# A hybrid decoder step on one core: one half of an SSM table moved to an earlier group, and the C and state rows loaded in an earlier block

## The chip, the cores and the metric

One NeuronCore of a Trainium2 chip runs the whole program, in float32. The metric is device time in microseconds of one execution; lower is better. Before the change it was 1676.16 us, the median of three runs (1675.69 to 1676.87).

## The reference, cut to what matters

The program is one step of a decoder layer for 1024 prompt tokens and 32 sample tokens (8 sequences of 4). A combined projection feeds two token mixers, their outputs are gated and projected, and a mixture of experts follows.

```
proj = h @ w_in                                   # u (512) | q, k, v (3 groups x 4 heads x 64)
# SSM branch: x_t = Abar x_(t-1) + Bbar u_t, y = Re(C x) + D u
dt = exp(log_step); mag = exp(lr*dt); ab = mag*cos(li*dt) + i*mag*sin(li*dt)
bb = (ab - 1) / (lr + i*li) * b                   # complex, 32 groups x 64 states x 16 channels
# sample tokens start from state_ssm_re/_im (8, 32, 64); prompt tokens from zero
# attention: three groups, window 128/512/2048 and dilation 1/4/16, prompt and sample
w = softmax over the three groups of their log-sum-exp
attn = sum_g w_g * o_g
gates = sigmoid(h @ w_mgate + b_mgate)
merged = g_ssm * (ssm @ w_br_ssm) + g_attn * (attn @ w_br_attn)
x = x + gt1 * (merged @ w_out); x = x + gt2 * moe(norm(x)); y = rmsnorm(x)
```

The kernel handles the scan in chunks of L = 8 tokens. For it, it needs powers of Abar (0 to 8), a table "ba" of Abar^(7-j) Bbar (the input table: what each of the 8 tokens of a chunk injects into the state; real part `ba_re`, imaginary part `ba_im`, 128 x 2048 each), and a table "ca" of C Abar^j.

## The kernel before, in words

The kernel is written engine by engine in blocks. All engines meet at the end of a block, so nothing of the next block starts before the slowest engine has finished this one. Within a block each engine works through its own list in the order written; semaphores join the lists. Four blocks matter here.

- **Projection block** (before 431 us): normalisation and the combined projection.
- **Prompt attention block** (lines 623 to 783). 24 units (3 groups x 8 tiles of 128 queries) go through PE (scores, transposed probabilities, values), DVE (mask, row maximum, half of the copies) and ACT (exponentials, other copies). SP loads two slabs of gate weights and then, for each unit, waits for the unit's output rows and stores them (L781). The rows sit in a ring of OB = 4 buffers `o_sb`; from unit 4 on, DVE's row maximum (L732, it writes into `o_sb`) waits until the store of four units before has landed. POOL writes zeros into the expert buffer (L634) and stores values (L650, L653).
- **Sample attention block** (lines 884 to 1299), the one that the change is about. Its parts:
  - SP starts it with the loads of the SSM parameters (L898 to L900, L903), then 32 loads of rows of C (L907), 2 loads of state rows (L910), and the caches of K and V of sample group 0 (L891). Later caches wait for the earlier group's use. After group 2 it stores the last sample rows, loads the rows of attention results of all tokens into `merge` (L928, L931).
  - PE has gate units as filler: `fill(step)` (L969) runs `FILL[step]` units of 8 matmuls of 128x352 at fixed points of its list, 30 units in all. Two units come first ("start"), then the transpose of the parameters (L976), one unit ("params"), then the wait for the 32 loads of C and the 2 of the states, their six transposes (L981, L983), three units ("c_h0"), and then for each sample group g: cache transposes (L997), scores (L1012, L1014), transposes (L1020, L1021, L1025, L1026), values (L1034, L1036), the transpose of the rows (L1041), with one unit in between each time. After group 2 nine units follow ("merge" 5, "merged" 4), then PE waits for the merged rows (`s_mrg`) and transposes them (L1052).
  - DVE computes the SSM constants, copies C and states out of PSUM (L1096 to L1099), and in each group does its copies and softmax steps. After the copy of the transposed probabilities (L1187, L1188) it runs one SSM piece: `powers` in group 0, `b_bar` in group 1, `b_table_re` in group 2. The adding of values (L1191) comes after the piece. After group 2: L1193, a memset (L1194), `b_table_im`, the chain table `e` (squarings and complex products, L1200 to L1221), then the merge of the three groups' rows (L1223 to L1245) and the copies of their transposes (L1249). The helper `tt` of L1061 records most of the products, so they all show as L1061.
  - POOL computes the table "ca" (L949 to L954) as soon as powers and C are there. ACT applies the bias to every gate unit and stores it (L1262, L1265), and computes the exponentials and sines between.
- **SSM block** (from L1340): transposes of the inputs, taps, injection with the tables `ba`, scan, output. The branch projections, router and experts follow in further blocks.

`big` is one buffer of 128 x 19584 that the stages share by column ranges. In the prompt attention, columns 0 to 18815 hold q, k and v. In the sample attention the turned caches `kct` use 14816 to 18911, and DVE's scratch for the tables is 10720 to 12767.

Of the kernel before, what the change touches and what calls it, by code (L numbers as in the profile page):

```python
# [38 lines left out]
SP2 = SSM_G // 2  # L39
# [36 lines left out]
def build(nc, I, O, scratch):  # L76
    ctx = ExitStack()
    with ctx:
# [5 lines left out]
        def sem(name):  # L84
            if front_sems is not None:
                s = nc.alloc_semaphore(name)
                front_sems.append(s)
                return s
            return ctx.enter_context(nc.semaphore(name))
# [15 lines left out]
        big = sb("big", [P, 19584])  # L105
# [37 lines left out]
        for blk in order:  # L143
            first_unit[blk] = len(units)
            kind, b = blk
# [452 lines left out]
        def place(rows, g, t):  # L598
# [4 lines left out]
                return rows[512 * (t // 4) + t % 4:512 * (t // 4 + 1):4]  # L603
            return rows[t:SEQ:8]

        OB = 4
        s_sc, s_msk, s_nm, s_p = sem("scores_in_psum"), sem("scores_masked"), sem("row_max_ready"), sem("probs_ready")
        s_gw = [sem(f"gate_weights{i}_loaded") for i in range(2)]
        s_zr, s_zst, s_vst = sem("zero_rows_ready"), sem("zero_rows_stored"), sem("v_stored")
        s_pt, s_pta, s_ptd = sem("probs_t_in_psum"), sem("probs_t_copied_act"), sem("probs_t_copied_dve")  # L610
        s_pv, s_o, s_st = sem("values_in_psum"), sem("values_copied"), [sem(f"att_rows_stored{i}") for i in range(OB)]

# [4 lines left out]
        with ExitStack() as st:  # L617
            s_sb = sb("s_sb", [P, 2, HEADS, 2 * P], stack=st)
            p_sb = sb("p_sb", [P, 2, HEADS, 2 * P], stack=st)
            pt_sb = sb("pt_sb", [P, 2, 2, HEADS, P], stack=st)  # L620
            o_sb = sb("o_sb", [P, OB, HEADS, HD + 2], stack=st)

            with nc.Block() as block:  # L623
# [91 lines left out]
                def _(dve):  # L715
                    V = nc.vector
                    for i in range(NU + 1):
                        if i < NU:
# [10 lines left out]
                            dve.wait_ge(s_msk, i + 1)  # L729
                            if i >= OB:  # L730
                                dve.wait_ge(s_st[i % OB], 16 * (i // OB))
                            V.tensor_reduce(o_sb[:, i % OB, :, HD].rearrange("p (k r) -> p r k", r=2),  # L732
                                            s_sb[:, i % 2, :, 0:w], AX.X, ALU.max, negate=True).then_inc(s_nm, 1)
# [10 lines left out]
                def _(act):  # L744
                    A = nc.scalar
                    for i in range(NU + 2):
                        if i < NU:
# [4 lines left out]
                            for s in range(HEADS):  # L752
                                h = 2 * (s % 2) + s // 2
                                m = A.activation(p_sb[:, i % 2, s, 0:w], s_sb[:, i % 2, s, 0:w], ACT.Exp,  # L754
                                                 bias=o_sb[:, i % OB, h, HD:HD + 1], scale=1.0,
                                                 accum_out=o_sb[:, i % OB, h, HD + 1:HD + 2])
# [15 lines left out]
                @block.sync  # L772
                def _(sp):
                    for b in range(2):
                        sp.dma_start(ring[:, b, :].rearrange("p (k c) -> p k c", k=KT),
                                     I["w_mgate"][0][:, b * WB:(b + 1) * WB].rearrange("(k p) c -> p k c", p=P)).then_inc(s_gw[b], 16)
                    for u, (g, t) in enumerate(att):
                        sp.wait_ge(s_o, u + 1)
                        sp.wait_ge(s_p, u + 1)
                        dst = place(scratch["att_rows"].rearrange("n g h d -> n g (h d)")[:, g, :], g, t)  # L780
                        sp.dma_start(dst, o_sb[:, u % OB, :, :].rearrange("p h d -> p (h d)")).then_inc(s_st[u % OB], 16)  # L781
                    for i in range(OB):
                        sp.wait_ge(s_st[i], 16 * NU // OB)
# [49 lines left out]
                                            sem("max_factors"), sem("merged"))  # L833
        s_atp, s_ate = sem("attn_t_in_psum"), sem("attn_t_copied")
        s_dve3, s_pool3 = sem("dve_chain3"), sem("pool_chain3")
        s_pl, s_bl, s_cl, s_hl = sem("ssm_params_loaded"), sem("ssm_b_loaded"), sem("ssm_c_loaded"), sem("ssm_h0_loaded")
        s_dtr, s_pt4, s_ct4 = sem("step_rows_ready"), sem("params_in_psum"), sem("c_in_psum")
        s_a1, s_a2, s_a3, s_a4 = sem("dt_ready"), sem("exponents_ready"), sem("magnitudes_ready"), sem("angles_ready")
        s_a5 = sem("sines_ready")
# [15 lines left out]
        with ExitStack() as st:  # L855
# [2 lines left out]
            rp = big[:, 1536:1792].rearrange("p (i j n) -> p i j n", i=2, j=L)  # L858
            par_rows = big[0:48, 1792:1920]
            ls = big[0:48, 1920:1922]  # L860
            h_rows4 = big[:, 10432:10688].rearrange("p (a c) -> p a c", a=2)
            c_rows4 = big[:, 18912:19424].rearrange("p (a c) -> p a c", a=4)
            g_sb = sb("gate_units", [P, GB, CW], stack=st)
            vc = sb("vc", [P, 4096], stack=st)
            st_sb = sb("st_sb", [P, 3, P], stack=st)
# [18 lines left out]
            with nc.Block() as block:  # L884
                @block.sync
                def _(sp):
                    def load_cache(src, dst, s, g):
                        rows = src[0].rearrange("n s h d -> n s (h d)")
                        if g < 2:
                            for b in range(KB[g]):  # L890
                                sp.dma_start(dst[:, :, b, :], rows[:, b * P:(b + 1) * P, :].rearrange("n s c -> s n c")).then_inc(s, 16)  # L891
                        else:

                            for a in range(16):
                                sp.dma_start(dst[4 * a:4 * a + 4, :, 0, :],
                                             rows[:, 16 * a:16 * a + 4, :].rearrange("n s c -> s n c")).then_inc(s, 16)

                    sp.dma_start(par_rows[0:16, :], I["ssm_a_re"][0].rearrange("(n r) s -> n (r s)", r=2)).then_inc(s_pl, 16)  # L898
                    sp.dma_start(par_rows[16:32, :], I["ssm_a_im"][0].rearrange("(n r) s -> n (r s)", r=2)).then_inc(s_pl, 16)
                    sp.dma_start(ls[32:48, :], I["ssm_log_step"][0].rearrange("(n r) -> n r", r=2)).then_inc(s_pl, 16)  # L900
                    for i, nm_ in enumerate(("ssm_b_re", "ssm_b_im")):
                        for r in range(2):
                            sp.dma_start(b_raw[64 * r:64 * r + 64, i, :, :],  # L903
                                         I[nm_][0].rearrange("(n r) s c -> r s n c", r=2)[r]).then_inc(s_bl, 16)
                    for i, nm_ in enumerate(("ssm_c_re", "ssm_c_im")):
                        for n in range(SP2):
                            sp.dma_start(c_rows4[16 * (n % 8):16 * (n % 8) + 16, 2 * i + n // 8, :].rearrange("c (r s) -> c r s", r=2),  # L907
                                         I[nm_][0, 2 * n:2 * n + 2].rearrange("r c s -> c r s")).then_inc(s_cl, 16)
                    for i, nm_ in enumerate(("state_ssm_re", "state_ssm_im")):
                        sp.dma_start(h_rows4[:, i, :], I[nm_][0].rearrange("b (n r) s -> (b n) (r s)", r=2)).then_inc(s_hl, 16)  # L910
                    for g in range(GROUPS):
                        if g:
                            sp.wait_ge(s_ktp, kt_before[g])
                        load_cache(I[caches[g][0]], kcv[g], s_kc[g], g)
                        if g:
                            sp.wait_ge(s_op, g)
                        load_cache(I[caches[g][1]], vcv[g], s_vc[g], g)
                        if g:
                            sp.wait_ge(s_or, g)
                            for h in range(HEADS):  # L920
                                sp.dma_start(scratch["att_rows"][SEQ:N, g - 1, h, :], d_sb[h * NS:(h + 1) * NS, :]).then_inc(s_ost, 16)
                    sp.wait_ge(s_or, GROUPS)
                    for h in range(HEADS):
                        sp.dma_start(scratch["att_rows"][SEQ:N, GROUPS - 1, h, :], d_sb[h * NS:(h + 1) * NS, :]).then_inc(s_ost, 16)
                    sp.wait_ge(s_clr, 1)
                    for m_, (_, t0, t1) in zip(merge, MERGE):
                        t1 = min(t1, TT)
                        sp.dma_start(m_[:, 0:t1 - t0].rearrange("p t g h d -> p t (g h d)"),  # L928
                                     scratch["att_rows"][t0 * P:t1 * P].rearrange("(t p) g h d -> p t (g h d)", p=P)).then_inc(s_all, 16)
                    sp.wait_ge(s_ost, 64 * GROUPS)  # L930
                    sp.dma_start(merge[1][0:NS, TT - 5].rearrange("p g h d -> p (g h d)"),  # L931
                                 scratch["att_rows"][SEQ:N].rearrange("n g h d -> n (g h d)")).then_inc(s_all, 16)

                    for i in range(GB):
                        sp.wait_ge(s_gst[i], 16 * (EARLY_UNITS // GB))
# [120 lines left out]
                def _(dve):  # L1056
                    V = nc.vector
                    c = Counted(s_dve3)
# [99 lines left out]
                    def b_table_im():  # L1158
                        tt(ba_im, rp_re, bb_im, ALU.mult)
                        tt(tmp4, rp_im, bb_re, ALU.mult)  # L1160
                        tt(ba_im, ba_im, tmp4, ALU.add)
# [4 lines left out]
                    for g in range(GROUPS):  # L1166
# [19 lines left out]
                        dve.wait_ge(s_ptp, g + 1)  # L1186
                        V.tensor_copy(pt2[0:w, 0:KB[g], :], bank[1][0:w, 0:KB[g] * P].rearrange("p (b c) -> p b c", c=P))  # L1187
                        V.tensor_copy(pt2[0:NS, 2, :], bank[1][0:NS, 256:384]).then_inc(s_pte, 1)  # L1188
                        (powers, b_bar, b_table_re)[g]()
                        dve.wait_ge(s_oa, g + 1)  # L1190
                        V.tensor_tensor(o2[:, :], o2[:, :], bank[3][0:HD, 0:P], ALU.add).then_inc(s_os, 1)  # L1191
                        dve.wait_ge(s_orp, g + 1)
                        V.tensor_copy(d_sb[:, 0:HD], bank[3][:, 256:256 + HD]).then_inc(s_or, 1)  # L1193
                    V.memset(merge[1][:, TT - 5].rearrange("p g h d -> p (g h d)"), 1.0).then_inc(s_clr, 1)  # L1194
                    b_table_im()

                    k = 0
                    src = (co, si)
# [47 lines left out]
                    for t in range(NT):  # L1246
                        dve.wait_ge(s_atp, t + 1)
                        r = rows_of(t)
# [1392 lines left out]
```

## Time and profile before

| | us |
|---|---|
| device time, median of 3 runs | 1676.16 |
| device time of the profiled execution | 1686.48 |
| its span (first to last instruction) | 1684.6 |
| PE busy | 1515.9 (90%) |
| DVE busy | 488.4 (29%) |
| ACT busy | 285.6 (17%) |
| POOL busy | 111.7 (7%) |

The profiled execution takes 10.3 us more than the median of the plain runs, of which 1.9 us lie outside the span. Stage times below are from it. The page also divides the span into 40 slices of 42.1 us: the prompt attention lies in slices 11 to 13, the sample attention in slices 14 to 19 (556 to 797 us).

### The profile page before, as it was taken

The page shows a single profiled execution, that of the slowest core. Times are in us where ns is not written, and L with a number is a line of the kernel's source. Part 1 is how long each engine was busy: PE and PEld are TensorE (multiplying, and loading weights), DVE is VectorE, ACT ScalarE, POOL GpSimd, SP SyncE. Part 2 cuts the span into 40 slices and gives each one's busy share as a digit, 9 for nine tenths or more (in the row PEclk, how much of TensorE's full clock was granted, in tenths as well). Part 3 has the DMA queues.
Part 4 walks back from the last instruction along what each step waited for, and adds up shares of the span by engine and source line. Part 5 has one row for each costly group of instructions (what it writes and reads, how often), then busy time and mean ns, then how long its engine had stood idle before and what let it go on. Part 6 is the DMA issues. An engine that isn't in the chain of part 4 may idle for free. (4 is left out here: it accounts for less than half of the span.)

```text
span 1684.6 us, 20319 instructions
## 1 busy us (share of the span) xinstructions
PE 1515.9 (90%) x8509; PEld 1011.6 (60%) x8509; DVE 488.4 (29%) x1064; ACT 285.6 (17%) x647; POOL 111.7 (7%) x113
## 2 busy tenths in 40 slices
PE   5999999999899799997999998999996799999940
PEld 3556569899778566764666666667886333333310
DVE  4300001110444111258009123433366241111108
ACT  4100000000445110001222112211112111111103
POOL 0000000000020004000100000000000100000023
PEclk9899999999766797898899999999997799999975
DMA  9342242200461333030232003832004699999948
GB/s 306 99 150 75 77 148 89 65 17 0 163 233 66 94 101 101 32 136 29 65 56 76 9 9 131 282 98 93 39 25 190 216 372 383 414 417 412 362 138 246
DMA packets 131422, 253.18 MB, mean 150 GB/s; under 512 B 22506, under 2 KB 96890, under 8 KB 123123
## 3 DMA queue, kind: packets, MB, share of 16 engines
q1 hardware_dynamic: 106082, 189.67, 32.0%
q0 software_dynamic: 10560, 33.50, 6.0%
q10 hardware_dynamic: 14688, 28.71, 4.5%
q8 instruction: 68, 1.11, 0.3%
q14 instruction: 24, 0.19, 0.0%
HBM read 204.96 MB, written 49.63 MB: 151 GB/s over the span
## 5 line engine op out<-in xcount | busy, mean ns | idle before, releaser
L351 PE MATMUL psum<-h_t,ring 128*128 128x352 f32 x576 | 174.1, 464 | 2.7 <-DVE h_t L510 2.7
L369 PE MATMUL psum<-ring,h_t 128*128 128x256 f32 (+1 forms) x720 | 171.8, 397 | 0.0
L969 PE MATMUL psum<-h_t,ring 128*128 128x352 f32 x480 | 164.3, 504 | 5.2 <-PEq L623 2.7
L369 PEld LDWEIGHTS psum<-ring,h_t 128*128 128x128 f32 (+1 forms) x720 | 155.1, 284 | 12.9 <-issue 2.4
L351 PEld LDWEIGHTS psum<-h_t,ring 128*128 128x128 f32 x576 | 110.2, 192 | 65.4 <-issue 6.4
L969 PEld LDWEIGHTS psum<-h_t,ring 128*128 128x128 f32 x480 | 99.2, 210 | 61.8 <-issue 17.8
L2046 PE MATMUL psum<-ring,big 128*128 128x256 f32 (+1 forms) x576 | 131.2, 388 | 2.1 <-PEq L1703 2.1
L2046 PEld LDWEIGHTS psum<-ring,big 128*128 128x128 f32 (+1 forms) x576 | 105.5, 185 | 22.9 <-issue 3.2
L2133 PE MATMUL psum<-w_gate_up,u_rows 128*32 128x512 f32 x608 | 101.7, 609 | 3.3 <-DMA w_gate_up<-in_w_exp_up 1.4
L2133 PE MATMUL psum<-ring,u_rows 128*32 128x512 f32 x576 | 101.7, 599 | 0.9 <-ACT u_rows L2254 0.9
L2155 PE MATMUL psum<-big 128*32 128x512 f32 x736 | 83.7, 595 | 0.8 <-DVE big L2555 0.8
L385 DVE COPY big<-psum 128x352 f32<-128x352 f32 (+1 forms) x30 | 14.5, 485 | 230.2 <-PE psum L351 150.5
L1744 PE MATMUL psum<-big,w_br_ssm 128*128 128x352 f32 x192 | 60.8, 460 | 1.4 <-ACT u_rows L1755 1.4
L701 PE MATMUL psum<-big,pt_sb 128*128 128x64 f32 x280 | 52.7, 360 | 8.9 <-ACT pt_sb L764 8.0
L701 PEld LDWEIGHTS psum<-big,pt_sb 128*128 128x128 f32 x280 | 48.9, 268 | 17.9 <-issue 13.3
L386 ACT ACTIVATE big<-psum 128x352 f32<-128x352 f32 (+1 forms) x30 | 12.9, 431 | 265.6 <-PE psum L351 176.7
L2133 PE MATMUL psum<-big,u_rows 128*32 128x512 f32 x288 | 56.5, 594 | 0.2 <-DMA w_gate_up<-in_w_exp_up 0.2
L2133 PEld LDWEIGHTS psum<-w_gate_up,u_rows 128*32 128x32 f32 x608 | 27.1, 112 | 48.7 <-issue 47.1
L2548 DVE SCALAR_TENSOR_TENSOR big<-big,weight_of_slot,psum 128x256 f32<-128x256 f32 x23 | 11.1, 481 | 150.7 <-ACT big L2260 150.7
L2133 PEld LDWEIGHTS psum<-ring,u_rows 128*32 128x32 f32 x576 | 26.1, 111 | 40.0 <-issue 38.9
L754 ACT ACTIVATE p_sb<-s_sb,o_sb 128x128 f32<-128x128 f32 (+1 forms) x96 | 42.1, 439 | 46.9 <-DVE o_sb L732 46.9
L1744 PEld LDWEIGHTS psum<-big,w_br_ssm 128*128 128x128 f32 x192 | 36.4, 190 | 21.7 <-ACT u_rows L1755 1.6
(460 smaller groups left out, 1885.9 us busy)
## 6 DMA issues: line engine op xcount, KB each, us to landing
big<-in_w_exp_down SPq DMA_DIRECT2D x32, 1024.0 KB, 9.3
ring<-in_w_ada SPq DMA_DIRECT2D x24, 1024.0 KB, 7.2
w_gate_up<-in_w_exp_gate SPq DMA_DIRECT2D x13, 1024.0 KB, 13.3
w_gate_up<-in_w_exp_up SPq DMA_DIRECT2D x13, 1024.0 KB, 17.3
ring<-in_w_exp_gate SPq DMA_DIRECT2D x13, 1024.0 KB, 10.5
ring<-in_w_exp_up SPq DMA_DIRECT2D x13, 1024.0 KB, 13.8
tmp_expert_rows<-ring POOLq DMA_DIRECT2D x12, 1024.0 KB, 4.4
ring<-in_w_in SPq DMA_DIRECT2D x11, 1024.0 KB, 8.4
```

The lines of the kernel that those rows point to most:

```text
L351: m = nc.tensor.matmul(bank[(e + j) % NB][:, 0:CW], w[:, k, c * P:(c + 1) * P], ht3[:, k, j * CW:(j + 1) * CW], start=(k == 0), stop=(k == ...
L369: m = nc.tensor.matmul(bank[e % NB][0:rows_of(t), 0:WB], lhs, w[:, k, :], start=(k == 0), stop=(k == KT - 1))
L385: return nc.vector.tensor_copy(dst, view)
L386: return nc.scalar.activation(dst, view, ACT.Copy)
L701: m = nc.tensor.matmul(bank[6 + u % 2][:, h * HD:(h + 1) * HD], pt_sb[:, u % 2, kb, slot, :], v_rows[:, g, tile, h * HD:(h + 1) * HD], sta ...
L754: m = A.activation(p_sb[:, i % 2, s, 0:w], s_sb[:, i % 2, s, 0:w], ACT.Exp, bias=o_sb[:, i % OB, h, HD:HD + 1], scale=1.0, accum_out=o_sb[ ...
L969: m = T_.matmul(bank[4 + u % 4][:, 0:CW], w_[:, k, c0:c0 + P], ht3[:, k, j * CW:(j + 1) * CW], start=(k == 0), stop=(k == KT - 1))
L1744: T_.matmul(bank[b0 + 2][:, 0:CW], w_bs[:, k, m_ * P:(m_ + 1) * P], y2_t[:, k, tok], start=(k == 0), stop=(k == 3))
L2046: m = T_.matmul(bank[2 * (i % 2) + b // 2][0:r, (b % 2) * WB:(b % 2 + 1) * WB], merged_t[:, k, t * P:t * P + r], w[:, k, :], start=(k == 0 ...
L2133: m = T_.matmul(bank[i][at, :], x_t[i][:, k * P + CHUNK * c:k * P + CHUNK * (c + 1)], w_gu[use_of(e, GSLOTS)[0]][:, :, k, :], start=(k == ...
L2155: m = T_.matmul(bank[4 + f][at, :], turned(hid_t[b % 2])[:, k, at], w_dn[use_of(e, DSLOTS)[0]][:, k, f * 512:(f + 1) * 512], start=(k == 0 ...
L2548: V.scalar_tensor_tensor(out=hid[b % 2], in0=sil[b % 2], scalar=w_slot[:, b:b + 1], in1=bank[b % 2][:, FF:2 * FF], op0=ALU.mult, op1=ALU.m ...
```

## The change

The loads of rows of C move from the start of the sample attention into the prompt attention: SP issues two (real and imaginary part of a pair of channel groups) before each of the first 16 units' stores, 32 in all. The two loads of the states go there too, ahead of the first unit. Both destinations move to columns of `big` above those that the prompt attention uses. On DVE, group 1 now runs `b_bar` and `b_table_re` behind one another, group 2 runs `b_table_im`, and the call of `b_table_im` behind the memset of L1194 is gone. The instructions themselves are the same and as many.

```diff
+        c_rows4 = big[:, 18816:19328].rearrange("p (a c) -> p a c", a=4)
+        h_rows4 = big[:, 19328:19584].rearrange("p (a c) -> p a c", a=2)
+        s_cl, s_hl = sem("ssm_c_loaded"), sem("ssm_h0_loaded")
@@ prompt attention, SP
                                      ... w_mgate loads
+                    for i, nm_ in enumerate(("state_ssm_re", "state_ssm_im")):
+                        sp.dma_start(h_rows4[:, i, :], I[nm_][0].rearrange("b (n r) s -> (b n) (r s)", r=2)).then_inc(s_hl, 16)
                     for u, (g, t) in enumerate(att):
+                        if u < SP2:
+                            for i, nm_ in enumerate(("ssm_c_re", "ssm_c_im")):
+                                sp.dma_start(c_rows4[16 * (u % 8):16 * (u % 8) + 16, 2 * i + u // 8, :].rearrange("c (r s) -> c r s", r=2),
+                                             I[nm_][0, 2 * u:2 * u + 2].rearrange("r c s -> c r s")).then_inc(s_cl, 16)
                         sp.wait_ge(s_o, u + 1)
@@ sample attention
-            h_rows4 = big[:, 10432:10688].rearrange("p (a c) -> p a c", a=2)
-            c_rows4 = big[:, 18912:19424].rearrange("p (a c) -> p a c", a=4)
@@ SP
-                    for i, nm_ in enumerate(("ssm_c_re", "ssm_c_im")):
-                        for n in range(SP2):
-                            sp.dma_start(c_rows4[...], I[nm_][0, 2 * n:2 * n + 2].rearrange("r c s -> c r s")).then_inc(s_cl, 16)
-                    for i, nm_ in enumerate(("state_ssm_re", "state_ssm_im")):
-                        sp.dma_start(h_rows4[:, i, :], ...).then_inc(s_hl, 16)
@@ DVE
-                        (powers, b_bar, b_table_re)[g]()
+                        for piece in ((powers,), (b_bar, b_table_re), (b_table_im,))[g]:
+                            piece()
                         ...
                     V.memset(merge[1][:, TT - 5]..., 1.0).then_inc(s_clr, 1)
-                    b_table_im()
```

## Rows read from the trace of the kernel before

**Rows 1.** The page: granted PE clock in 40 slices, in tenths of full speed.

```profile
PEclk9899999999766797898899999999997799999975
```

**Rows 2.** Waits, 556 to 800 us: engine, line, releaser: total, times, longest.

```profile
PE psum L1052 <- DVEq L1245: 10.2, 1, 10.2
```

**Rows 3.** Timeline, SP, 553 to 600 us: start, length, line, transfer, [idle before].

```profile
561.31 7.70 SPq L907 DMA_DIRECT2D big<-in_ssm_c_re  x16
...
576.53 0.42 SPq L910 DMA_DIRECT2D big<-in_state_ssm_re  x1
...
577.47 0.66 SPq L891 DMA_DIRECT2D big<-in_cache_k_w  x1
```

**Rows 4.** Timeline, PE, 548 to 640 us.

```profile
569.64 5.00 PE L969 MATMUL psum<-h_t,ring 128*128 128x352 f32 x16
579.46 0.90 PE L981 MATMUL psum<-ident,big 128*128 128x128 f32 x4 [4.82 <-DMA big<-in_state_ssm_im]
...
580.58 15.61 PE L969 MATMUL psum<-h_t,ring 128*128 128x352 f32 x48
596.03 1.04 PE L997 MATMUL psum<-ident,big 128*128 128x128 f32 x8
...
599.45 5.00 PE L969 MATMUL psum<-h_t,ring 128*128 128x352 f32 x16 [0.79 <-DVE big L1172]
604.29 1.85 PE L1012 MATMUL psum<-q_pair,big 128*128 128x8 f32 x16
...
609.56 7.09 PE L969 MATMUL psum<-h_t,ring 128*128 128x352 f32 x16
```

**Rows 5.** Stretches, all engines: busy by engine, granted PE clock, DMA share, GB/s.

```profile
580.00:586.00 6.00, 6.00 (x19) 3.93 (x18) 2.32 (x7) 0.00 (x0) 0.00 (x0) 0.74 0.96 324
...
640.00:646.00 6.00, 4.98 (x33) 3.43 (x33) 4.94 (x9) 0.55 (x1) 5.92 (x2) 1.00 0.14 40
...
784.00:790.00 6.00, 0.00 (x0) 0.00 (x0) 5.90 (x4) 0.00 (x0) 0.00 (x0) 0.54 0.00 0
```

**Rows 6.** Timeline, DVE, 640 to 800 us.

```profile
683.48 0.42 DVE L1061 TENSOR_TENSOR b_bar_c<-b_bar_c,tmp_pow 128x256 f32<-128x256 f32 x1
...
740.01 2.23 DVE L1061 TENSOR_TENSOR ring<-big,b_bar_c 128x2048 f32<-128x2048 f32 x1
...
746.93 0.17 DVE L1061 TENSOR_TENSOR ssm_small<-ssm_small 128x16 f32<-128x16 f32 x1
...
775.64 0.27 DVE L1227 TENSOR_REDUCE merge_tot<-big 128x20 f32<-128x60 f32 x1
...
790.68 1.23 DVE L1244 TENSOR_TENSOR vc<-vc,big 128x1024 f32<-128x1024 f32 x1
```

**Rows 7.** Timeline, PE, 640 to 805 us.

```profile
699.07 0.27 PE L1041 MATMUL psum<-ident,o 64*128 64x64 f32 x1
...
738.93 42.87 PE L969 MATMUL psum<-h_t,ring 128*128 128x352 f32 x144
```

**Rows 8.** Timeline of SP, then of ACT, 735 to 800 us.

```profile
742.12 0.47 SPq L931 DMA_DIRECT2D big<-tmp_att_rows  x1
...
762.90 0.56 ACT L1262 ACTIVATE gate_units<-psum,prm_t 128x352 f32<-128x352 f32 x1 [4.18 <-PE psum L969]
```

**Rows 9.** Prompt attention, SP: waits (425 to 560 us), then issues of L781.

```profile
SPq L781 <- ACT o_sb L769: 109.2, 24, 8.5
...
L781 SPq DMA_DIRECT2D tmp_att_rows<-o_sb x24: 319/320/339, 444.9 to 554.8; - x24
...
DMA to landing us min/median/max: 1.7/1.7/5.5
```

**Rows 10.** Issues by transfer, 556 to 800 us: count, KB each, median us to landing.

```profile
big<-in_cache_k_w SPq DMA_DIRECT2D x3, 1024.0 KB, 7.5
...
big<-in_ssm_c_re SPq DMA_DIRECT2D x16, 8.0 KB, 1.7
...
big<-tmp_att_rows SPq DMA_DIRECT2D x1, 99.0 KB, 10.6
```

More of the change, by code:

```diff
@@ L835, in build @@
         s_dve3, s_pool3 = sem("dve_chain3"), sem("pool_chain3")
-        s_pl, s_bl, s_cl, s_hl = sem("ssm_params_loaded"), sem("ssm_b_loaded"), sem("ssm_c_loaded"), sem("ssm_h0_loaded")
+        s_pl, s_bl = sem("ssm_params_loaded"), sem("ssm_b_loaded")
         s_dtr, s_pt4, s_ct4 = sem("step_rows_ready"), sem("params_in_psum"), sem("c_in_psum")
@@ L904, in _ @@
                                          I[nm_][0].rearrange("(n r) s c -> r s n c", r=2)[r]).then_inc(s_bl, 16)
-                    for i, nm_ in enumerate(("ssm_c_re", "ssm_c_im")):
-                        for n in range(SP2):
-                            sp.dma_start(c_rows4[16 * (n % 8):16 * (n % 8) + 16, 2 * i + n // 8, :].rearrange("c (r s) -> c r s", r=2),
-                                         I[nm_][0, 2 * n:2 * n + 2].rearrange("r c s -> c r s")).then_inc(s_cl, 16)
-                    for i, nm_ in enumerate(("state_ssm_re", "state_ssm_im")):
-                        sp.dma_start(h_rows4[:, i, :], I[nm_][0].rearrange("b (n r) s -> (b n) (r s)", r=2)).then_inc(s_hl, 16)
                     for g in range(GROUPS):
```

## The prediction

> **What bounds the kernel now.** I read the page first. PE is busy for 1515.9 of 1684.6 us, so only what makes PE wait or run slowly can move the time. The line of granted clock [rows 1] shows where it is slow: the prompt attention and the sample attention (slices 11 to 18, digits 6 to 9) are below full speed. Then I read the waits of the sample attention, because the diff touches that block and its neighbour. The longest wait of PE there is 10.2 us before the transposes of the merged rows (L1052), and its releaser is DVE [rows 2]. The second is 4.82 us before L981, and its releaser is the load of the states [rows 4]. Between the two PE has only short gaps. So this block ends as late as PE's list, plus one wait for SP's loads near its start, plus one wait for DVE at its end. Each half of the change addresses one of these waits.
>
> Next I read the timeline of each engine that ends such a wait. For SP the reader is to see one long row of issues: the 32 loads of C are issued from 561.31 to 576.53 us, 0.47 us each, and the states only behind them [rows 3]. A load of C lands 1.7 us after its issue [rows 10], so it is the issuing that takes the time and not the bytes. For DVE the reader is to see a list without gaps after group 2: from 740.01 us the three products of `b_table_im`, then the chain table, then the merge, to 790.68 + 1.23 = 791.91 us [rows 6]. PE has finished its nine filler units at 738.93 + 42.87 = 781.80 us [rows 7] and sits idle.
>
> **Part one, the loads.** PE's unit before the transposes starts at 569.64 us. A unit at full clock gives way to the next instruction 604.29 - 599.45 = 4.84 us after its start [rows 4]. With C and states loaded long before, L981 starts at 569.64 + 4.84 = 574.48 in place of 579.46: 4.98 us gained.
>
> The wait has a second cost. The three units behind it take 596.03 - 580.58 = 15.45 us [rows 4], while nine units at the end of the block take 42.87, so three take 14.29. The first of the three ran partly at the lower level: the granted clock is 0.74 in 580 to 586 us, a mixture of 2.4 and 1.2 GHz, after the idle stretch ahead of it [rows 5]. Without the idle stretch I take 15.45 - 14.2 = 1.25 us more, 14.2 being three units at the 4.74 us that ACT's evenly spaced units show (4.18 idle and 0.56 busy, [rows 8]). The ends for this term are 0 (the clock falls all the same) and 1.5. Sum of part one: 4.98 + 1.25 = 6.23 us.
>
> The Trainium skill ("TensorE: Matmul & The Clock Gate", Part 4, PE-mode transpose) says that transposes do not count as PE activity for the clock. By that rule the six transposes might let the clock fall by themselves and the 1.25 would be 0, a total of 1664.3. The trace speaks against it: 640 to 646 us is almost all transposes (L997) and the granted clock stays 1.00 [rows 5]. I go by the row.
>
> What else could end last there? The transposes of cache K of group 0 (L997) would come at about 596.03 - 6.23 = 589.8 us. Its load is issued today at 577.47 [rows 3] and is 7.5 us on the way [rows 10]. Its issue moves up with the 34 loads that leave SP's list, to about 561.3, so it lands near 570. DVE's copies of C and states and its query pairs run beside the three units, 14 us of cover for some ten short instructions. The later caches wait for PE's own progress and shift with it.
>
> In the prompt attention SP gets 32 x 0.47 + 2 x 0.43 = 16 us of issues [rows 3]. It waits there for 109.2 us in total for ACT's outputs [rows 9], and the stores come (554.8 - 444.9) / 23 = 4.78 us apart [rows 9]. A unit adds 2 x 0.47 = 0.94 us of issue, put before the wait for that unit's output, so the store itself is not late. Even if it were, DVE asks for the store's landing only four units (19 us) after it, and it takes 1.7 us, 5.5 at most [rows 9]. The last eight units have no load, so the block's end is as today. Cost 0; if the cover were gone, see the second rival.
>
> **Part two, the table.** `b_table_im` leaves the end of DVE's list: 746.93 - 740.01 = 6.92 us [rows 6]. Everything after it on DVE is one chain up to the merge, so the merge ends 6.92 us earlier relative to the end of group 2. In its place group 1 gets `b_table_re`, also three products of 128x2048, 6.9 us. `b_bar` ends at 683.48 + 0.42 = 683.90 [rows 6], so the table ends at about 690.8. The next piece of DVE that PE needs is the sum of L1191 for the transpose L1041, which runs only at 699.07 [rows 7]: 8 us of margin. Group 2 has a table of the same size in the same place as today. Cost 0; if PE got to L1041 more than 8 us sooner, the excess would be paid there.
>
> What is late next at the block's end? Take the 6.23 us of part one off everything. PE ends its filler at 775.6, DVE the merge at 791.91 - 6.23 - 6.92 = 778.8. DVE is still last, by 3.2 us, so all 6.92 count. The merge's rows must be there by 775.64 - 13.15 = 762.5 [rows 6]; the last of these loads is issued at 742.12 [rows 8] and lands 10.6 us later [rows 10], at 753, or 747 with the shift. ACT must have passed its fifth unit after group 2, which today it does at 762.90 + 0.56 = 763.5 [rows 8], 757.2 with the shift, while DVE asks for its factors about 1 us after it has the rows, at 763.5. Both hold.
>
> With 3.2 us idle in place of 10.2 the clock may fall later: today it is 0.54 on average in 784 to 790 us, that is, it fell some 2.7 us after PE had stopped at 781.80 [rows 5, 7]. The eighteen transposes then alternate with DVE's copies; with the full clock they could gain up to 1 us. I take 0.
>
> **Sum.** 6.23 + 6.92 = 13.15 us. For the profiled execution that is 1686.48 - 13.15 = 1673.3; against the median 1676.16 - 13.15 = 1663.0 us. All later blocks start from the common end of this one and shift with it. What remains open is where the stretches at the lower clock fall after the shift: a filler unit takes 7.09 us in such a stretch and 5.00 outside [rows 4]. From the rows I give this 2 us more or less in the sample attention and another 1 or 2 in what follows: 3 to 4 in all.
>
> **Rivals.**
> 1. Only one wait goes. For: each half rests on one ending alone, and something unseen could take its place (a constant of DVE behind L981, a store before the merge). Against: the margins above are 8 to 16 us but for ACT's, which is some 6 us. Only the table pays: 1676.16 - 6.92 = 1669.2. Only the loads pay: 1676.16 - 6.23 = 1669.9.
> 2. Slower: SP becomes the pace of the prompt attention. The loads go ahead of the stores on one queue; a store that must stay behind two loads costs each of the 16 units their issue, 0.94 us, or a landing as well, 0.94 + 1.7 [rows 3, 10]. That adds 15 to 42 us and takes 13.15 away: 1678 to 1705, with one landing per unit (16 x 1.7 = 27.2) 1690.2. It decides only once loads and store need more than the 4.78 us of a unit for many units, since three further units of slack lie in the ring. Today's sum is 0.94 + 0.32 + 1.7 = 3 us. The Trainium skill ("DMA: Bandwidth & Descriptors", Issuing engines are not separate DMA queues) says that transfers of all engines interleave on the same 16 DMA engines, which is how POOL's zeros could stretch such a queue; the 5.5 us of the slowest store [rows 9] show some of it.
> 3. More than forecast: the clock stays high before L1052 and another low stretch is missed: 13.15 + 1 + 1.6 = 15.75, or 1660.4. The 1.6 is what the stretch from 580 to 586 us loses against full clock, (1 - 0.74) x 6 [rows 5].
> 4. The change does not do what it says, a wait for the loads stays at L981 since the loads of the new place land late: the last is issued at unit 15, some 35 us before the block. Practically excluded.
>
> **Chances.** Forecast, within its own 1660.5 to 1666: 0.70. More than forecast: 0.10. A smaller gain between 1666 and 1671, rival 1 with the low stretches falling badly: 0.13. Below that, down to no change within 0.2% (3.4 us, about what a measurement tells from none): 0.04. Rival 2: 0.03. The range from 1658.5 to 1668.5 leaves out some 0.15 to 0.2. Faster by over 0.2% is 0.94, within 0.2% 0.03, slower 0.03.
>
> **What would show it.** In the profile after: no wait for a DMA at L981, and its row about 4.8 us after the start of the unit before; three units behind it in 14.3 us; the first cache load of SP issued near 561 us; three 2048-wide products behind `b_bar` in group 1, with L1041 of group 1 not waiting; the wait at L1052 down from 10.2 to about 3.2 us; the last store of the prompt attention 109.9 us after the first, as before. The prediction is wrong if that stretch is longer by over 1 us, if PE waits elsewhere in groups 0 to 2, or if the wait at L1052 stays near 10.

## The result, and the profile after

The changed kernel takes 1657.38 us (median of six runs, 1652.83 to 1668.94); the kernel before takes 1677.32 over the six runs beside it. The ratio is 0.9896, with a 95% interval from 0.9865 to 0.9928: faster by 12 to 23 us. I had predicted 1663.0 (13.15 us of gain) within 1658.5 to 1668.5. Over all 28 runs of this kernel taken for this study the mean is 1659.3 us, over 87 runs of the kernel before it is 1677.0: a gain of 17.7 us with a standard error of 1.6.

The profiled execution has a span of 1660.2 us where the one before had 1684.6. I cut both at the same three points: PE's first scores of the prompt attention, its first filler unit of the sample attention, its first transpose of the SSM block.

| stretch, us | before | after | difference |
|---|---|---|---|
| up to the prompt attention | 431.91 | 431.59 | -0.3 |
| prompt attention | 125.15 | 117.96 | -7.2 |
| sample attention | 240.79 | 227.10 | -13.7 |
| rest | 886.75 | 883.55 | -3.2 |

So the block for which the gain was worked out gives what was worked out, and 10.7 us more have come elsewhere: 7.2 in the prompt attention, where the change only adds loads on SP, and 3.2 behind the block. First the waits of PE in the sample attention after, for which [rows 2] stood before; the lines of code are one to three further down in this kernel (L1053 is the old L1052, L970 the old L969).

```profile
PE psum L1053 <- DVEq L1246: 3.3, 1, 3.3
PE psum L970 <- PEq L626: 2.7, 1, 2.7
PE psum L1477 <- DMA big<-tmp_u_new: 2.5, 1, 2.5
PE psum L970 <- DVE big L1173: 2.5, 3, 0.9
```

The wait for DVE ahead of the merged rows is down from 10.2 to 3.3 us, and no wait for the states is left. PE's timeline at the start of the block, for [rows 4]:

```profile
562.14 5.00 PE L970 MATMUL psum<-h_t,ring 128*128 128x352 f32 x16
566.98 0.60 PE L982 MATMUL psum<-ident,big 128*128 128x128 f32 x4
567.42 0.38 PE L984 MATMUL psum<-ident,big 128*128 128x128 f32 x2
567.64 14.37 PE L970 MATMUL psum<-h_t,ring 128*128 128x352 f32 x48
581.84 1.04 PE L998 MATMUL psum<-ident,big 128*128 128x128 f32 x8
```

The transposes follow the unit before by 4.84 us, and the three units take 581.84 - 567.64 = 14.20 us in place of 15.45. From the start of the unit before to the first transposes of K (L998) it is 581.84 - 562.14 = 19.70 us, where it was 596.03 - 569.64 = 26.39: 6.69 us less. DVE's timeline in group 1 and at the end of the block, for [rows 6]:

```profile
669.28 0.43 DVE L1062 TENSOR_TENSOR b_bar_c<-b_bar_c,tmp_pow 128x256 f32<-128x256 f32 x1
669.74 2.29 DVE L1062 TENSOR_TENSOR ring<-big,b_bar_c 128x2048 f32<-128x2048 f32 x1
672.07 2.29 DVE L1062 TENSOR_TENSOR big<-big,b_bar_c 128x2048 f32<-128x2048 f32 x1
674.39 2.29 DVE L1062 TENSOR_TENSOR ring<-ring,big 128x2048 f32<-128x2048 f32 x1
678.93 0.28 DVE L1193 TENSOR_TENSOR o<-o,psum 64x128 f32<-64x128 f32 x1 [2.24 <-ACT o L1294]
...
769.48 1.22 DVE L1245 TENSOR_TENSOR vc<-vc,big 128x1024 f32<-128x1024 f32 x1
```

The moved table ends at 676.7, and DVE still waits 2.24 us for ACT before its sum: the table cost nothing in group 1. The merge ends at 770.70, and PE, done with its nine filler units, follows at 770.82:

```profile
724.70 42.87 PE L970 MATMUL psum<-h_t,ring 128*128 128x352 f32 x144
770.82 5.25 PE L1053 MATMUL psum<-ident,vc 128*128 128x128 f32 x18 [3.26 <-DVEq L1246]
776.65 6.43 PE L1472 MATMUL psum<-ident,u_rows 128*128 128x128 f32 x32 [0.58 <-PEq L891]
```

From the first of the nine filler units to the next block it is 776.65 - 724.70 = 51.95 us, where it was 797.85 - 738.93 = 58.92: 6.97 us less. With the 6.69 us at the start that makes 13.66 of the 13.7 us, so the two waits are all of the difference in this block.

SP in the prompt attention (some of its issues, then its first cache load in the next block; the two lines of the loads of C are L785, the stores L790):

```profile
432.60 1.68 SPq L781 DMA_DIRECT2D big<-in_state_ssm_re  x1
434.32 0.76 SPq L781 DMA_DIRECT2D big<-in_state_ssm_im  x1
435.12 0.43 SPq L785 DMA_DIRECT2D big<-in_ssm_c_re  x1
435.60 0.42 SPq L785 DMA_DIRECT2D big<-in_ssm_c_im  x1
444.54 0.34 SPq L790 DMA_DIRECT2D tmp_att_rows<-o_sb  x1
...
477.93 1.25 SPq L785 DMA_DIRECT2D big<-in_ssm_c_re  x1
479.23 0.82 SPq L785 DMA_DIRECT2D big<-in_ssm_c_im  x1
...
554.87 0.66 SPq L898 DMA_DIRECT2D big<-in_cache_k_w  x1
```

The cache load is now issued 5.3 us after the block's start in place of 20.4. What SP waited for in the prompt attention, for [rows 9]:

```profile
SPq L790 <- ACT o_sb L772: 79.4, 24, 8.4
```

What is different in the prompt attention itself is PE's clock. One row for each kernel over this stretch (columns as in [rows 5]), before and then after:

```profile
431.30:556.60 125.30, 112.10 (x612) 94.40 (x612) 56.51 (x67) 61.86 (x235) 17.99 (x29) 0.65 0.43 158
```

```profile
431.60:549.50 117.90, 103.70 (x612) 86.67 (x612) 56.13 (x65) 61.34 (x235) 17.95 (x29) 0.72 0.47 172
```

The same 612 records of matmuls take 8.4 us less of PE's time, with a granted clock of 0.72 in place of 0.65, while DVE, ACT and POOL do the same work in the same time.

### The profile page after: what moved, and what is told of

It reads as the page before. It is cut to its first block and busy times, and to the rows that moved or that the text cites. A ratio compares the mean times of both kernels' runs of the same rounds, so it can differ in the third digit from the quotient of the medians.

```text
span 1660.2 us, 20319 instructions
## 1 busy us (share of the span) xinstructions
PE 1502.4 (90%) x8509; PEld 1000.5 (60%) x8509; DVE 488.1 (29%) x1064; ACT 285.4 (17%) x647; POOL 113.2 (7%) x113
## 5 line engine op out<-in xcount | busy, mean ns | idle before, releaser
L970 PE MATMUL psum<-h_t,ring 128*128 128x352 f32 x480 | 162.6, 500 | 5.1 <-PEq L626 2.7
L970 PEld LDWEIGHTS psum<-h_t,ring 128*128 128x128 f32 x480 | 98.2, 208 | 61.0 <-issue 16.0
L385 DVE COPY big<-psum 128x352 f32<-128x352 f32 (+1 forms) x30 | 14.5, 485 | 230.0 <-PE psum L351 150.3
L704 PE MATMUL psum<-big,pt_sb 128*128 128x64 f32 x280 | 47.3, 333 | 10.1 <-ACT pt_sb L767 9.2
L704 PEld LDWEIGHTS psum<-big,pt_sb 128*128 128x128 f32 x280 | 43.7, 242 | 19.0 <-issue 14.6
## 6 DMA issues: line engine op xcount, KB each, us to landing
ring<-in_w_exp_up SPq DMA_DIRECT2D x13, 1024.0 KB, 13.5
```

Source lines behind the costliest of these rows:

```text
L704: m = nc.tensor.matmul(bank[6 + u % 2][:, h * HD:(h + 1) * HD], pt_sb[:, u % 2, kb, slot, :], v_rows[:, g, tile, h * HD:(h + 1) * HD], sta ...
L970: m = T_.matmul(bank[4 + u % 4][:, 0:CW], w_[:, k, c0:c0 + P], ht3[:, k, j * CW:(j + 1) * CW], start=(k == 0), stop=(k == KT - 1))
```

## The experiments

My theory, A below: the gain is the sum of the two waits, and what goes beyond it is a clock that varies from execution to execution. The rival, B: the loads of C, now in the prompt attention, move its low-clock stretches and so shorten it.

**1. The two parts apart, the whole again, and loads without use.** `e1_loads_only` is the changed kernel with this undone:

```diff
-                        for piece in ((powers,), (b_bar, b_table_re), (b_table_im,))[g]:
-                            piece()
+                        (powers, b_bar, b_table_re)[g]()
 ...
+                    b_table_im()
```

> Only the 34 loads move; the imaginary table stays behind the memset. Theory A (the gain is the two waits, and what lies beyond 13.15 us is a granted clock that varies from execution to execution): 6.2 us under the kernel before, no wait for a load ahead of the six transposes, 10.2 us of wait ahead of the transposes of the merged rows; the time of the prompt attention (125.3 us before, 118.0 after) may be anything between these. Theory B (the loads themselves shorten the prompt attention, by shifting its low-clock stretches): 11 to 13 us under the kernel before and a prompt attention near 118 us.

`e2_table_only` is the kernel before with the same lines the other way round.

> Only the imaginary table moves to group 2 and the real one to group 1; all loads stay at the start of the sample attention. Theory A: 6.9 us under the kernel before, wait ahead of the transposes of the merged rows 3.3 us in place of 10.2, wait of 4.8 us for the states as before; prompt attention anywhere between 118 and 126 us. Theory B: also 6.9 us, but the prompt attention at 125 us since no load runs in it.

`e3_after_again` is the changed kernel.

> The changed kernel once more, beside the others on one chip. Theory A: 13 us under the kernel before (1663 against 1676) and the profile's prompt attention anywhere between 118 and 126 us; the device time of the runs goes with their mean clock. Theory B: 17 to 20 us under, prompt attention again near 118 us.

`e4_extra_loads` is the kernel before with the new SP lines added and the old ones kept; at the end of the block SP also waits until the extra loads have landed:

```diff
+                    for i, nm_ in enumerate(("state_ssm_re", "state_ssm_im")):
+                        sp.dma_start(h_rows_x[:, i, :], ...).then_inc(s_hlx, 16)
                     for u, (g, t) in enumerate(att):
+                        if u < SP2:
+                            ...  sp.dma_start(c_rows_x[...], ...).then_inc(s_clx, 16)
```

> The kernel before, with a second copy of the 34 loads in the prompt attention (into unused columns), the original loads and the tables unmoved; nothing uses the second copy. Theory A: no change beyond 0.2% and a prompt attention between 118 and 126 us. Theory B: 4 to 7 us faster, prompt attention near 118 us. A third way, that the loads disturb the stores (my rival 2): slower by 15 us or more.

Measured, as ratio to the kernel before on the same chip: loads alone 0.9954 (0.9928 to 0.9979), table alone 0.9956 (0.9930 to 0.9983), both 0.9887 (0.9848 to 0.9927), extra loads 1.0008 (0.9983 to 1.0032). The last speaks against B and against my rival 2 at once: the loads next to the stores neither gain nor cost, within some 3 us one way and 5 the other. `e1` speaks against B too, with a prompt attention of 127.0 us. Only `e3` came out as B had it: its runs have a mean of 1657.0 us (standard error 3.3), 19 us under the kernel before, and its prompt attention takes 117.0 us. The traces of the parts each lack just one wait. Loads alone: three units at full clock, and the wait for DVE as before.

```profile
576.52 14.37 PE L970 MATMUL psum<-h_t,ring 128*128 128x352 f32 x48
...
783.17 5.24 PE L1053 MATMUL psum<-ident,vc 128*128 128x128 f32 x18 [10.21 <-DVEq L1246]
```

Table alone: the wait for the states and the slow first unit are there, and the wait for DVE is short.

```profile
576.92 0.87 PE L981 MATMUL psum<-ident,big 128*128 128x128 f32 x4 [4.81 <-DMA big<-in_state_ssm_im]
578.02 15.63 PE L969 MATMUL psum<-h_t,ring 128*128 128x352 f32 x48
...
782.48 5.25 PE L1052 MATMUL psum<-ident,vc 128*128 128x128 f32 x18 [3.23 <-DVEq L1245]
```

One thing stayed open: both profiles of the whole change had a short prompt attention (118 and 117 us), the four others 125 to 127. `e1` has exactly the same instructions up to there, so this looked like chance, but two of two asked for more profiles.

**2. More profiles, another place of the loads, and a shorter chain.** `e6_after_third` is the changed kernel, `e7_before_profile` the kernel before.

> The changed kernel a third time, for one more profile and more runs. If the short prompt attention (118 and 117 us in its two profiles, 125 to 127 in four profiles of other kernels) is chance, it may be either here; if it belongs to this kernel it is 117 to 118 again. Device time 1658 plus or minus 7.

> The kernel before once more, for a second profile. Prompt attention 125 us if that length belongs to the kernel, anything from 117 to 127 if it is chance. Device time 1676.

The third profile of the changed kernel has the longest prompt attention of all, 129.97 us at a clock of 0.59, the second had the shortest, 117.01 at 0.76. Over that stretch, `e3_after_again`, then `e6_after_third`:

```profile
429.50:546.50 117.00, 101.11 (x613) 84.48 (x613) 56.10 (x65) 61.30 (x235) 17.92 (x29) 0.76 0.48 173
```

```profile
429.60:559.60 130.00, 119.74 (x613) 100.39 (x613) 56.49 (x65) 61.87 (x235) 17.98 (x29) 0.59 0.43 156
```

So the short prompt attention does not belong to the kernel. The fourth profile of the changed kernel, `e10` below, says it from the other side. Here are the kernel before and `e10` over their prompt attention, the one without and the other with the loads:

```profile
431.91:557.06 125.15, 112.10 (x612) 94.39 (x613) 56.23 (x65) 61.82 (x235) 17.95 (x29) 0.65 0.43 159
```

```profile
431.81:556.98 125.17, 112.11 (x612) 94.41 (x613) 56.23 (x65) 61.85 (x235) 17.96 (x29) 0.65 0.44 162
```

Length, PE's busy time and clock are the same. The four runs of `e6` have a mean of 1654.1 us (standard error 4.4; ratio 0.9854, 0.9819 to 0.9889), inside the 1658 plus or minus 7.

`e7`, the kernel before against itself, had a prompt attention of 124.4 us and a ratio of 1.0024 with an interval of 1.0003 to 1.0045, which leaves out 1. One interval in twenty does that by chance, so one case doesn't show that the intervals are too narrow; I count nothing under 0.3% as a difference.

`e8_loads_up_front` issues all loads of C before the first store:

```diff
-                    for u, (g, t) in enumerate(att):
-                        if u < SP2:
+                    for u in range(SP2):
                             for i, nm_ in enumerate(("ssm_c_re", "ssm_c_im")):
                                 sp.dma_start(c_rows4[...], ...).then_inc(s_cl, 16)
+                    for u, (g, t) in enumerate(att):
                         sp.wait_ge(s_o, u + 1)
```

> The changed kernel with all 32 loads of C issued before the first unit's store in place of two ahead of each of 16 stores. If the place of the loads within the prompt attention has nothing to do with its length: as the changed kernel, 1658 within 4 us, first store some 5 us later than today and DVE not waiting for it. If loads spread among the stores shift the low-clock stretches: prompt attention back to 125 us and 5 to 7 us slower than the changed kernel.

Ratio 0.9938 (0.9909 to 0.9968), mean 1665.3 us, 6 us (standard error 2.3) above the changed kernel's. That is the size that I had given for a shift of low-clock stretches, but its prompt attention is 124.1 us, within what the changed kernel has in its own profiles, and the trace shows a cost of another kind. The expectation that DVE would not wait was wrong. SP's first store comes at 452.96 us in place of 444.54, and three of DVE's row maxima wait for stores to land, which none did in the other kernels. SP's timeline, then DVE's wait (total, times, longest):

```profile
452.96 14.86 SPq L790 DMA_DIRECT2D tmp_att_rows<-o_sb  x4
```

```profile
DVE o_sb L735 <- DMA tmp_att_rows<-o_sb: 4.5, 3, 3.1
```

This is the mechanism of my rival 2, called up by bunching the loads: up to 4.5 us. How much of these reaches PE is not shown, and at one clock (the table below) `e8` is only 2.8 us above the changed kernel; so the wait is shown, and its share of the 6 us is not.

`e5_chain_early` takes 9.5 us more out of DVE's list behind group 2:

```diff
-                        for piece in (..., (b_table_im,))[g]:
+                        for piece in (..., (b_table_im, squares))[g]:       # the three squarings
                             piece()
                         ...                                                # the sum of values
+                        if g == 2:
+                            chain_start()                                  # the two memsets of e
+                            chain_steps(8)                                 # doublings of widths 1, 2, 4
                         dve.wait_ge(s_orp, g + 1)
```

> The changed kernel with 9.5 us more of DVE's list taken from behind group 2: the three squarings go behind the imaginary table in group 2 (2.5 us into 3.3 us of idle time), the first three doublings of the chain table go between the sum of values and the copy of rows of group 2 (7.0 us into 7.2). Theory A (PE waits for DVE at the block's end and for nothing else): the wait of 3.2 us ahead of the transposes of the merged rows goes, DVE now waits about 4 us for ACT's factors, and the time is 3 to 4 us under the changed kernel, 16 us under the kernel before. Rival (PE's filler or ACT's stores end the block as late): no change against the changed kernel.

The wait ahead of L1053 is gone and the granted clock stays 1.00 from 760 to 768.3 us, so that the transposes behind it take 4.1 us in place of 5.3. DVE waits 3.8 us for ACT's factors, as expected. PE's timeline:

```profile
720.99 42.87 PE L970 MATMUL psum<-h_t,ring 128*128 128x352 f32 x144
763.69 0.60 PE L1053 MATMUL psum<-ident,vc 128*128 128x128 f32 x4
764.59 0.77 PE L1053 MATMUL psum<-ident,vc 128*128 128x128 f32 x4 [0.30 <-DVE big L1262]
...
768.34 1.06 PE L1484 MATMUL psum<-ident,u_rows 128*128 128x128 f32 x8 [0.58 <-PEq L891]
...
777.33 3.59 PE L1489 MATMUL psum<-ident,big 16*128 16x16 f32 x32 [3.84 <-DMA big<-tmp_u_new]
```

From the first of the nine units to the next block it takes 768.34 - 720.99 = 47.35 us in place of 51.95 in the changed kernel (776.65 - 724.70): 4.6 us gained on the spot, where 3 to 4 were expected. Its runs don't show it: ratio 0.9907 (0.9873 to 0.9941), a mean of 1660.5 us.

**3. The last two once more, side by side.** `e9_chain_again` is `e5`, `e10_after_fourth` the changed kernel.

> The kernel with the early chain steps once more, beside the changed kernel on the same chip. In its first profile the stretch from the first filler unit behind group 2 to the next block was 47.4 us against 52.0 in the changed kernel, yet its runs were not faster. If the 4.6 us are real and the runs only hide them: mean of its runs 3 to 5 us under that of the changed kernel here, or within the scatter of 2 to 3 us of that. If something later gives them back: no difference in the mean, and the stretch behind the block longer in its profile again (886 us against 880 to 884 in others).

> The changed kernel a fourth time. Its first 16 runs have a mean of 1657 us, the kernel before 1677 over 66, and the two parts alone gain 7 and 6. If the sum of the two waits (13.15 us) is all of the gain, the mean of these runs comes out nearer to 1664; if a better clock in this kernel belongs to it, it stays at 1657 with a mean clock of 0.918.

Ratios 0.9925 (0.9895 to 0.9955) and 0.9914 (0.9883 to 0.9945). The twelve runs of `e10` have a mean of 1662.3 us (standard error 2.2) at a mean clock of 0.9148: nearer to 1664 than to 1657, as expected if the two waits are all of the gain and the better clock of the first 16 runs was chance. The runs of `e9` have a mean of 1663.7 us (1.8), 1.5 above it in place of 3 to 5 below. The shorter chain doesn't win, and its rest behind the block is 886.1 and 886.2 us in its two profiles, where the changed kernel has 883.6, 879.4, 880.2 and 883.4. A part of it is plain: in the next block PE waits for the rows of `u` anyway (3.84 us where the changed kernel waits 2.55), and the small transposes behind that wait run at the lower clock, 3.59 us where the changed kernel has 2.44. The remainder lies in the taps and injection, where the time takes one of three values in all profiles (199.5 to 199.8, 202.4 to 202.5 or 205.4 to 205.5 us from the first late gate unit that reads `u_rows` to the first product with `w_br_ssm`; the kernel before alone had 205.5 and 199.5). With two profiles I can't say whether the shorter chain draws the longer ones. It is no proven improvement.

All runs together, with the mean granted clock of the execution. The column "at one clock" is from a fit with one level for each kernel and one common slope, which is -1.06 us per 0.001 of clock:

| kernel | runs | mean us (standard error) | mean clock | at clock 0.910 |
|---|---|---|---|---|
| before | 87 | 1677.0 (0.5) | 0.9112 | 1678.2 |
| before, extra loads (e4) | 12 | 1677.1 (1.4) | 0.9101 | 1677.2 |
| loads only (e1) | 12 | 1669.8 (1.7) | 0.9109 | 1670.8 |
| table only (e2) | 12 | 1670.7 (1.9) | 0.9123 | 1673.2 |
| changed | 28 | 1659.3 (1.5) | 0.9165 | 1666.2 |
| changed, loads up front (e8) | 12 | 1665.3 (1.8) | 0.9135 | 1669.0 |
| changed, chain early (e5, e9) | 20 | 1662.1 (1.5) | 0.9139 | 1666.2 |

And the stretches of all profiles:

| profile | prompt attention, us (clock) | sample attention, us (clock) | rest |
|---|---|---|---|
| before; e7 | 125.2 (0.65); 124.4 (0.65) | 240.8 (0.85); 236.1 (0.88) | 886.8; 882.3 |
| e4 | 126.4 (0.61) | 236.8 (0.87) | 879.6 |
| e1 | 127.0 (0.61) | 230.1 (0.87) | 879.1 |
| e2 | 125.2 (0.65) | 233.8 (0.87) | 884.1 |
| after; e3; e6; e10 | 118.0 (0.72); 117.0 (0.76); 130.0 (0.59); 125.2 (0.65) | 227.1 (0.87); 219.0 (0.91); 223.2 (0.88); 227.1 (0.87) | 883.6; 879.4; 880.2; 883.4 |
| e8 | 124.1 (0.68) | 219.1 (0.91) | 881.4 |
| e5; e9 | 120.3 (0.71); 128.8 (0.61) | 218.3 (0.90); 222.3 (0.88) | 886.1; 886.2 |

## Why the prediction was right where it was, and where not

**Part one, the loads: right.** The start of the transposes was forecast 4.84 us after the unit before, and is. The slow first unit was forecast to cost 1.25 us, and the three units take 14.20 in place of 15.45. Uncounted were the six transposes themselves, which ran in the low stretch too: 0.66 us from the first to the next unit in place of 1.12. With these 0.46 us part one gave 6.69 us on the spot against 6.23. The runs of the loads alone gain 7.2 us (standard error 1.8) against 6.23. The Trainium skill ("TensorE: Matmul & The Clock Gate", Part 4, PE-mode transpose) says that transposes do not count as PE activity in the same way. By that rule I could have taken 0 for the 1.25. The trace bears out the choice against it: the granted clock is 1.00 in every stretch from 561 to 582 us, through the six transposes and the three units behind them. Six transposes of less than a microsecond together say little of the rule itself.

**Part two, the table: right.** The wait at the block's end was to fall to 3.2 us and is 3.26, and 3.23 to 3.27 in the three other profiles of the kernel. The price in group 1 was to be 0 and is; PE does not wait at L1042. The runs of the table alone gain 6.3 us (standard error 2.0) against 6.92. The sample attention of the profiled execution shrinks by 13.7 us where 13.15 were forecast. Over the profiles of the three executions with neither part its mean is 237.9, over the five with both (e8 among them) 223.1.

**The issues in the prompt attention: right that they are covered, wrong in size.** I had 16 us of issue. In the profiled execution the 32 issues of C last 21.3 us together and the two of the states 2.4. SP's wait for ACT fell by more, from 109.2 to 79.4 us, since the whole stretch was 7 us shorter too; in `e10`, whose stretch is as long as before, it is 89.7 us, with 20.6 us of issues. The rows on which the 0.47 us rested are of another stretch; here a load of C takes up to 1.6 us to issue, and 2.5 to 2.7 us (median) to land in place of 1.7. SP had room for that. The point from which rival 2 decides is nearer than I wrote, as `e8` shows: not many units that lack time, but one delay of the first store by 8 us. And the sign that I had named for being wrong, first to last store of the prompt attention longer than 109.9 us by over 1 us, is no sign of SP's pace: in `e6` it is 114.8 us with DVE waiting for no store, and in the profiled execution 102.8.

**The transposes at the end: 0 was taken, up to 1 us was left open.** They took 5.25 us in the profiled execution, where the clock fell inside the wait of 3.26 us, and 4.7 in `e3` and `e8`, where it was 1.00 through the first eight or so and fell to 0.50 behind them.

**The step that failed is the last term of the sum, "3 to 4 us in all" for where the low stretches fall.** The sum itself, 13.15 us, holds: the block gave 13.7. The uncertainty put on it was too small. I took it from the length of single filler units in the sample attention. Measured on one kernel, the sample attention varies by 8 us (219.0 to 227.1), the prompt attention by 13 (117.0 to 130.0), and I had not counted the prompt attention at all since nothing was gained or lost there by an edit. The device times of the changed kernel go from 1644.2 to 1670.1 us with the clock of the execution, the correlation is -0.94. The three runs of before that I had, within 1.2 us of each other, hid this: 87 runs have a standard deviation of 4.8 us. The 28 runs of the changed kernel have 7.7. My range held the mean of all runs by 0.8 us, and the median of the first six lies 1.1 us below its lower end. Both lie in the branch "more than forecast", to which I had given 0.10. Its first term, the clock staying high before the transposes, is seen only in `e3` and `e8` and is worth 0.5 us there; its second, one more low stretch missed at 1.6 us, is of the right kind and too small. That the range holds the mean is in part luck.

**What the excess is.** The runs of the two parts gain 13.5 us together (standard error 2.7), near the 13.15; the whole gains 4.2 us more than these (2.9), which is not clear of scatter. At one clock the parts gain 7.4 and 5.0, together 12.4, and the whole 12.0. That column errs low, since the change itself takes time at the low level out of the program: the idle time before L1052, and the first unit after L981. From 6.9 us less at 0.50 ahead of L1052 and 3.4 us less at 0.50 around L981 (579.7 to 583.1 us in the profile before) I estimate that this alone raises the mean clock by 0.0024, which the fit then counts as 2.5 us of clock. So 12 to 15 us belong to the two waits. The rest goes with a mean clock of 0.9165 in place of 0.9112, of which the 0.0024 explain about half. Against the explanation that the other half belongs to the kernel stand the four profiles of its prompt attention, from 117.0 to 130.0 us for one list of instructions, and `e10`, where the clock was 0.9148 and the gain 14.5 us. For it stands that 28 runs have a standard error of 0.0012 in the clock. I leave that open.

## What to carry to other kernels

Where PE's list is one chain with filler, look for the few waits of PE that are not its own rhythm, and ask of each whether the issue, the bytes or the order on the other engine ends it; here the 34 issues of SP and the order of DVE's list did, and in the traces both edits paid their full length because a spare gap was there to take the work. A wait costs more than its idle time if what follows runs at the low clock: a start 4.98 us late cost 6.7 in all. And before calling a gain of less than one per cent, take ten runs or more of each kernel and set them beside the granted clock; three runs can agree by chance, and one profile can be short by chance. A mean at one clock is a help and no more, since an edit that takes out slow time changes the clock too.

## What the runs showed of the hardware that was not expected

- One list of instructions runs at a mean granted clock between 0.59 and 0.76 in the prompt attention, from execution to execution, with PE busy 119.7 or 101.1 us for it. In this stretch PE works in short groups with gaps of 1 to 2 us and its clock changes level several times; what decides where, no run here shows.
- Over whole executions 0.001 of mean clock is worth 1.06 us, with a scatter of 2.8 us about the line.
- Issuing a load of C (8 KB) from SP took longer near POOL's 1 MB stores. In the eight profiles with the loads spread, the 24 issues that came within 5 us after such a store was issued have a mean of 0.61 to 0.79 us; the other eight have 0.43 to 0.46, but for 0.58 in the first profile of the changed kernel, which holds one of 1.59 us with no such store near. The longest took 1.99 us (`e3`). That the stores are the cause is not shown.
